# The last job of each output phase taken tile by tile in two banks, with most of the sums of squares inside its products

## The reference

```
x = x + gated_deltanet_mixer(rms_norm(x, a_norm_g), a_w_in, ...)      # phases A and OUT_A
x = x + moba_mixer(rms_norm(x, b_norm_g), b_w_in, w_out, kb, vb, ...) # phases B and OUT_B; kb, vb from rms_norm(x, kv_norm_g) @ w_kv
x = rms_norm(x, final_norm_g)
h = rms_norm_f32(x, norm_g) * (1 + scale) + shift                     # shift, scale, gate = silu(c) @ ada_w + ada_b
x = x + gate * retention_mixer(h, ...)                                # phases C and OUT_C
h = rms_norm_f32(x, norm_g) * (1 + scale) + shift
x = x + gate * chunked_attention_mixer(h, ...)                        # phases D and OUT_D
```

## Time and profile before

| | us |
|---|---|
| median of 3 runs | 833.12 |
| lowest and highest run | 832.19, 843.05 |
| the profiled execution's own time | 833.37 |
| its span | 831.5 |
| TensorE busy in the span | 814.4 |
| VectorE busy | 603.0 |
| ScalarE busy | 486.6 |
| GpSimd busy | 43.6 |

### The profile page before, as it was taken

The page is one execution under the profiler, slowest core; times in us unless marked ns, Lnnn a source line. Parts: engine busy times, 40 slices in busy tenths (PEclk is TensorE's granted clock), DMA queues, the critical chain, the costliest instruction groups (busy, mean ns, idle before and its releaser), DMA issues.

```text
span 831.5 us, 17292 instructions
## 1 busy us (share of the span) xinstructions
PE 814.4 (98%) x7278; PEld 793.7 (95%) x7278; DVE 603.0 (73%) x1049; ACT 486.6 (59%) x761; POOL 43.6 (5%) x68
## 2 busy tenths in 40 slices
PE   8999999999999999999999999989999999999998
PEld 7899999989999999999999999989999999999998
DVE  4776976678887876878797985556777867565662
ACT  5756756646855466553535354347777767677731
POOL 0500000018000100000000001000000000000000
PEclk9999999999999999999999999999999999999999
DMA  7363234526866884386666664973555644443450
GB/s 289 113 240 110 103 108 149 148 82 218 252 227 236 224 328 153 109 296 208 248 208 248 222 236 127 247 232 107 203 199 203 207 149 153 152 166 140 152 178 26
DMA packets 26493, 153.78 MB, mean 185 GB/s; under 512 B 2848, under 2 KB 3376, under 8 KB 12080
## 3 DMA queue, kind: packets, MB, share of 16 engines
q1 hardware_dynamic: 24432, 146.37, 50.3%
q0 software_dynamic: 1984, 6.31, 4.0%
HBM read 150.04 MB, written 2.62 MB: 184 GB/s over the span
## 4 chain that ended last, share of the span: by engine, by line
PE 84%; DVE 7%; DMA 4%; ACT 3%; issue 1%; SPq 0%; DVEq 0%; ACTq 0%
PE ps L489 83%; DMA raw<-weights 4%; DVE wlo L1444 3%; ACT whi L1013 1%; PE ps L869 1%; DVE early L1629 0%; DVE hlo L1472 0%; DVE arena L1476 0%; DVE early L1511 0%; DVE arena L1511 0%; DVE arena L1652 0%; DVE ada_ring L1525 0%; DVE olo L1489 0%; ACT hhi L1043 0%; PE ps L738 0%
## 5 line engine op out<-in xcount | busy, mean ns | idle before, releaser
L1444 DVE TENSOR_TENSOR wlo<-raw,whi 128x1024 fp32r<-128x1024 f32 x224 | 267.7, 1232 | 113.8 <-ACT whi L1013 113.8
L489 PE MATMUL ps<-hhi,whi 128*128 128x256 f32 x1024 | 295.0, 288 | 5.3 <-DVE hlo L1472 1.7
L489 PE MATMUL ps<-hlo,whi 128*128 128x256 f32 x1024 | 290.2, 283 | 0.0
L489 PE MATMUL ps<-hhi,wlo 128*128 128x256 f32 x1024 | 290.1, 283 | 0.0
L1013 ACT ACTIVATE whi<-raw 128x1024 fp32r<-128x1024 f32 x224 | 227.1, 1054 | 88.2 <-PE ps L489 60.9
L489 PEld LDWEIGHTS ps<-hhi,whi 128*128 128x128 f32 x1024 | 196.5, 192 | 8.2 <-issue 5.3
L489 PEld LDWEIGHTS ps<-hlo,whi 128*128 128x128 f32 x1024 | 196.7, 192 | 0.4
L489 PEld LDWEIGHTS ps<-hhi,wlo 128*128 128x128 f32 x1024 | 196.6, 192 | 0.0
L489 PE MATMUL ps<-ohi,whi 128*128 128x256 f32 x448 | 128.8, 287 | 1.4 <-DVE olo L1489 1.3
L489 PE MATMUL ps<-olo,whi 128*128 128x256 f32 x448 | 126.7, 283 | 0.0
L489 PE MATMUL ps<-ohi,wlo 128*128 128x256 f32 x448 | 126.7, 283 | 0.0
(11 more groups left out here) (232 smaller groups left out, 961.4 us busy)
## 6 DMA issues: line engine op xcount, KB each, us to landing
raw<-weights SPq DMA_DIRECT2D x112, 1024.0 KB, 5.0
ada_ring<-ada SPq DMA_DIRECT2D x24, 1024.0 KB, 5.1
arena<-bias_rows_d POOLq DMA_DIRECT2D x4, 512.0 KB, 15.8
x<-x_t SPq DMA_DIRECT2D x2, 512.0 KB, 4.7
arena<-bias_rows_b POOLq DMA_DIRECT2D x4, 256.0 KB, 7.8
bias_rows_d<-turns POOLq DMA_DIRECT2D x1, 1024.0 KB, 13.3
arena<-bias_rows_d POOLq DMA_DIRECT2D x4, 256.0 KB, 19.5
out_t<-x SPq DMA_DIRECT2D x4, 256.0 KB, 2.4
```

What stands on the lines that cost most here:

```text
L489: return pe.matmul(o, l, r, start=start, stop=stop, skip_group_check=skip)
L1444: dve.tensor_tensor(wlo[:, unit % UNITS, :, :], raw[:, c % RAW, 4 * half:4 * half + 4, :], whi[:, unit % UNITS, :, :].bitcast(F32), ALU.su ...
```

## The change

The last job of every output phase (19, 39, 67 and 103) is done by a new function, `job_by_tiles`. In its last chunk it takes all 24 products of tile 6 first, into the usual bank, and counts up tile_done; then the 24 of tile 7, into bank ps[6]. The units' slots are counted free in the second tile's products: the first unit's after k = 3 of tile 7, the second's at the end. VectorE adds tile 6 when tile_done comes, and tile 7 when the job is complete, each as one 128x256 instruction. ScalarE squares tile 6 on x6_ok and tile 7 on bank_free.

`x_sums` is split: `x_sums_begin` (ones products of tiles 0, 1 and 6) is issued in the last job behind its products k = 5 of tile 7, so that 6 products of the job come after it; `x_sums_end` (tile 7) stands where x_sums stood. The first unit of the chunk after the next moves: on VectorE from ahead of the addition to behind the addition of tile 7, on ScalarE from ahead of the squares to between the squares of tile 6 and tile 7. The low parts of the next chunk stay ahead of both additions. At the end tiles 6 and 7 of the result leave in a transfer each. Cut to its core:

```diff
-            for n in range(4):
+            for n in range(3):
                 J = JOB_OUT_D + n
                 sp.wait_ge(bank_free[J % 2], J // 2 - 5)
                 sp.dma_start(out[:, 2 * n:2 * n + 2, :], x[:, 2 * n:2 * n + 2, :]).then_inc(out_ok_sem, 16)
-            sp.wait_ge(out_ok_sem, 64)
+            sp.wait_ge(x6_ok_sem, 4)
+            sp.dma_start(out[:, 6, :], x[:, 6, :]).then_inc(out_ok_sem, 16)
+            sp.wait_ge(bank_free[(N_JOBS - 1) % 2], (N_JOBS - 1) // 2 - 5)
+            sp.dma_start(out[:, 7, :], x[:, 7, :]).then_inc(out_ok_sem, 16)
+            sp.wait_ge(out_ok_sem, 80)
...
+            def x_sums_begin(n):
+
+                pe.wait_ge(ss_read_sem, own_ss[0])
+                pe.wait_ge(xsq_add_sem, 2 * n)
+                pe.wait_ge(sq_ok_sem, 5 * n + 1)
+                for t in (0, 1, 6):
+                    mm(ssb[:, 0:S], ones[:, :], xsq[:, t, :], t == 0, False)
+
+            def x_sums_end(n):
+
+                pe.wait_ge(sq_ok_sem, 5 * n + 2)
+                mm(ssb[:, 0:S], ones[:, :], xsq[:, 7, :], False, True).then_inc(ss_ok_sem, 1)
+                own_ss[0] += 1
+
+            def job_by_tiles(J, between=None):
+
+                banks = (pj[J % 2], ps[6])
+                bank_empty(J)
+                cs = chunks_of(J)
+                for n, c in enumerate(cs):
+                    last = n == len(cs) - 1
+                    for t, k in [(t, k) for t in range(2) for k in range(KT)] if last else [(None, k) for k in range(KT)]:
+                        unit = 2 * c + k // 4
+                        if k % 4 == 0:
+                            pe.wait_ge(lo_ok_sem, unit + 1)
+                        for tile in range(2) if t is None else (t,):
+                            for a, (ws, hs) in enumerate(((whi, ohi), (whi, olo), (wlo, ohi))):
+                                m = mm(banks[tile][:, 0:S], ws[:, unit % UNITS, k % 4, tile * P:tile * P + P], hs[:, 8 * n + k, :],
+                                       n == 0 and k == 0 and a == 0, last and k == KT - 1 and a == 2)
+                        if t == 0 and k == KT - 1:
+                            m.then_inc(tile_done_sem, 1)
+                        elif t != 0 and k % 4 == 3:
+                            m.then_inc(w_units_sem, 1)
+                        if t == 1 and k == 5 and between is not None:
+                            between()
...
-            for J in range(JOB_OUT_A + 2, JOB_B):
-                job(J, "T", ohi, olo)
-
-            def x_sums(n):
-                pe.wait_ge(xsq_add_sem, 2 * n)
-                sums(lambda t: xsq[:, (0, 1, 6, 7)[t], :], 4, S, sq_ok_sem, lambda t: 4 * n - 2 + (3, 3, 4, 4)[t])
...
-                        job(J, "T", *h_q, ready=0, ready_sem=xg_lo_sem, at={4: lambda: x_sums(1)})
+                        job(J, "T", *h_q, ready=0, ready_sem=xg_lo_sem, at={4: lambda: x_sums_end(1)})
...
-            for J in range(JOB_OUT_B + 2, JOB_C):
-                job(J, "T", ohi, olo)
-
+            job(JOB_OUT_B + 2, "T", ohi, olo)
+            job_by_tiles(JOB_OUT_B + 3, lambda: x_sums_begin(2))
             ada_group(0)
-            x_sums(2)
+            x_sums_end(2)
...
-                    job(J, "T", ohi, olo)
-                ada_after(J)
+                    job_by_tiles(J, lambda: x_sums_begin(3))
             ada_group(1)
-            x_sums(3)
+            x_sums_end(3)
...
                     if n == 3:
-                        high(chunks_of(J0 + 4)[0] + 1, range(1))
+                        for t in (6, 7):
+                            if t == 6:
+                                act.wait_ge(x6_ok_sem, (JOB_OUT_A, JOB_OUT_B, JOB_OUT_C).index(J0) + 1)
+                            else:
+                                high(chunks_of(J0 + 4)[0] + 1, range(1))
+                                bank_taken(act, J)
+                            if J0 == JOB_OUT_A:
+                                act.activation(hhi[:, t, :], x[:, t, :], ACT.Copy, scale=col("b_norm", t)).then_inc(xg_hi_sem, 1)
+                            act.activation(xsq[:, t, :], x[:, t, :], ACT.Square, scale=1.0 if gain is None else gain(t)).then_inc(sq_ok_sem, 1)
+                        continue
...
-                        dve.wait_ge(sq_ok_sem, 4 * i + 2 + n)
+                        dve.wait_ge(sq_ok_sem, 5 * i + 2 + n)
...
-                    if n == 3 and J0 < JOB_OUT_D:
-                        low(chunks_of(J0 + 4)[0] + 1, range(1))
+
+                    def add_tile(t):
+
+                        k = 2 * n + t
+                        summed = ps[6][:, 0:S] if n == 3 and t else bank(J)[:, t, :]
+                        if gate is None:
+                            return dve.tensor_tensor(x[:, k, :], summed, x[:, k, :], ALU.add)
+                        return dve.scalar_tensor_tensor(out=x[:, k, :], in0=summed, scalar=mod[:, gate + k:gate + k + 1], in1=x[:, k, :], op0=ALU.mult, op1=ALU.add)
+
+                    def low_of_next(t):
+
+                        dve.wait_ge(xg_hi_sem, t + 1)
+                        dve.scalar_tensor_tensor(out=hlo[:, t, :], in0=x[:, t, :], scalar=col("b_norm", t), in1=hhi[:, t, :].bitcast(F32), op0=ALU.mult, op1=ALU.subtract).then_inc(xg_lo_sem, 1)
+
+                    if n == 3:
+                        i = (JOB_OUT_A, JOB_OUT_B, JOB_OUT_C, JOB_OUT_D).index(J0)
+                        dve.wait_ge(tile_done_sem, i + 1)
+                        add_tile(0).then_inc(x6_ok_sem, 1)
+                        if J0 == JOB_OUT_A:
+                            low_of_next(4)
+                            low_of_next(5)
+                            dve.wait_ge(x6_ok_sem, i + 1)
+                            low_of_next(6)
+                        sums_done(J)
+                        add_tile(1).then_inc(bank_free[J % 2], 1)
+                        if J0 == JOB_OUT_A:
+                            dve.wait_ge(bank_free[J % 2], J // 2 - 5)
+                            low_of_next(7)
+                        if J0 < JOB_OUT_D:
+                            low(chunks_of(J0 + 4)[0] + 1, range(1))
+                        continue
...
```

More of the change, by code:

```diff
@@ L358, in two_blocks @@
         ada_in_sem = sem("ada_in")
+        tile_done_sem = sem("tile_done")
+        x6_ok_sem = sem("x6_ok")
         bank_free = [sem(f"bank_free{i}") for i in range(2)]
@@ L530, in sums @@
                 for t in range(n):
-                    if cnt_sem is not None:
-                        pe.wait_ge(cnt_sem, cnt(t))
+                    pe.wait_ge(cnt_sem, cnt(t))
                     m = mm(ssb[:, 0:width], ones[:, :], src(t), t == 0, t == n - 1)
@@ L832, in _ @@
             ada(ADA_EARLY - 1)
-            for J in range(JOB_OUT_A + 2, JOB_B):
-                job(J, "T", ohi, olo)
-            def x_sums(n):
-                pe.wait_ge(xsq_add_sem, 2 * n)
-                sums(lambda t: xsq[:, (0, 1, 6, 7)[t], :], 4, S, sq_ok_sem, lambda t: 4 * n - 2 + (3, 3, 4, 4)[t])
+            job(JOB_OUT_A + 2, "T", ohi, olo)
+            job_by_tiles(JOB_OUT_A + 3, lambda: x_sums_begin(1))
             def head_sums(i, k):
@@ L980, in _ @@
                     job(J, "T", ohi, olo, split=8, at={4: lambda: sums_c(3)})
-                else:
-                    job(J, "T", ohi, olo)
-                ada_after(J)
+                elif J < JOB_D - 1:
+                    job(J, "T", ohi, olo)
+                else:
+                    job_by_tiles(J, lambda: x_sums_begin(3))
             ada_group(1)
-            x_sums(3)
+            x_sums_end(3)
             keep_warm(8)
@@ L991, in _ @@
                     job(J, "T", ohi, olo, split=16, at={8: turn_last, 12: mix_last})
+                elif J < N_JOBS - 1:
+                    job(J, "T", ohi, olo)
                 else:
-                    job(J, "T", ohi, olo)
+                    job_by_tiles(J)
         @block.scalar
@@ L1733, in add_x @@
                             low(J0 + 2, range(1, 2))
[L1734 to L1739, removed]
-                    else:
[L1741 to L1744, removed]
+                        if J0 == JOB_OUT_A and n:
+                            dve.wait_ge(bank_free[(J - 1) % 2], (J - 1) // 2 - 5)
+                            low_of_next(2 * n - 2)
+                            low_of_next(2 * n - 1)
+                    else:
+                        add_tile(0)
+                        add_tile(1).then_inc(bank_free[J % 2], 1)
             def attend(J0, pairs, soft0, bias, normed):
```

## The result

The changed kernel takes 838.53 us (median; 833.18 to 842.53 over 20 executions), the kernel before 833.25 us (830.49 to 843.05, 20 executions) beside it. The ratio is 1.0059, 95% interval 1.0046 to 1.0072: slower by 4.9 us, within 2%. The forecast was 838.7 us. The profiled execution of the changed kernel took 838.07 us, 835.9 of it in the span; that of before 833.37 and 831.5, so the spans differ by 4.4 us.

A forecast was written before the change was run, and what follows sets the result against it. The prediction took TensorE to bound the kernel, busy in 814.4 of 831.5 us. Its terms summed as 833.37 + 2.4 + 1.2 + 0.6 - 0.6 + 1.7 = 838.7 us, range 834.5 to 841.8.

The forecast's parts named there:

- The wait: In the last jobs of OUT_A, OUT_B and OUT_C, TensorE stands 3.2, 1.2 and 3.3 us for tile 6's square.
- OUT_A: End of OUT_A: the new wait, no longer covered by 24 products of B's first job, costs 2.4 us.
- OUT_B: End of OUT_B: TensorE never stood still there before, so the new wait is added whole, costing 1.2 us.
- The clock: Behind a long stall the granted clock falls once, taken at OUT_C, and slower instructions cost 1.7 us more.
- OUT_C: End of OUT_C: the earlier demand eats the gain meant there, costing 0.6 us without a clock fall.
- Rival 4: At OUT_C weights land 3.3 us sooner, removing stall and clock fall: no slower, 833.6 us; chance 0.10.
- The end: End of OUT_D: one shorter addition left and a smaller last transfer gain 0.6 us.
- Rival 3: At the output phases' ends, tile 6's additions come in time, nothing stalls: -4.2 us, 829.2 us; chance 0.05.

The follow-up runs named there:

- e1: Changed kernel with VectorE's addition of tile 6 ahead of the next chunk's low parts, and ScalarE's square ahead of its second high part: 830.04 us, ratio to before 0.9962.
- e2: Changed kernel with the ones sums of tiles 0, 1 and 6 put back behind the last job, additions still late: 830.59 us, ratio to before 0.9973.
- e7: Changed kernel with the edits of both e1 and e2: 829.5 us, ratio to before 0.9963.
- e4: Changed kernel with unneeded ones products on TensorE ahead of x_sums_begin in OUT_A, OUT_B and OUT_C (22, 8, 20 instructions): 842.74 us, ratio to before 1.0103.
- e8: Changed kernel with 16 unneeded ones instructions on TensorE ahead of x_sums_begin in OUT_A alone: 845.74 us, ratio to before 1.014.
- e10: Changed kernel run again with no edit, one execution, for a second trace: 838.31 us.
- e11: Changed kernel run again with no edit, one execution, for a third trace: 840.34 us.
- e3: Kernel before with only job 103 done tile by tile, tiles 6 and 7 added and sent apart: 832.47 us, ratio to before 1.0002.
- e6: Kernel before with only the third unit of OUT_A, OUT_B and OUT_C moved behind the last job's additions and squares: 832.55 us, ratio to before 0.9987.
- e9: Kernel before with the edits of e6 and e3 together: 830.38 us, ratio to before 0.997.

## Why the prediction was right, and where not

**The wait.** Right. It was foretold at three places with 3.2, 1.2 and 3.3 us, and is there with 2.83, 1.00 and 2.50, released by the square each time, with tile 6 added when the second wlo ends. e1, e2 and e7 remove it from either side and remove the loss.

**OUT_A.** +2.4 foretold without a fall of the clock, +2.28 and +2.29 with the stall filled (e4, e8). The cover named is the 24 products that now stand behind the wait. e2 shows it: its additions are as late, its sums wait behind those products again, and TensorE does not stand still there.

**OUT_B.** +1.2 foretold, +1.23 measured in all three traces of the changed kernel.

**The clock.** The step that failed is its place, "I take one such fall, at OUT_C": for the term of 1.7 us there the runs show 0. Of the ends of the output phases, one had a fall, OUT_A. The price of 1.7 us was near in the profiled execution (1.38) and in e10 (14.47 - 12.94 = 1.53), and too low in e11 (15.67 - 12.94 = 2.73). I had argued from the old fall at OUT_C and from the stall being longest there. The stall came out shorter there than at OUT_A (2.50 against 2.83), and the old fall stays with the old order (before and e3). That reading also said that the old trace had one fall; it has a second, from 46 to 50, in phase A. The Trainium skill, TensorE: Matmul & The Clock Gate, section "HAM oscillation — how this bites in real kernels", describes a loop that waits some 3 to 5 us for data between groups of matmuls and starts each group throttled again; the 3.2 and 3.3 us foretold lay at the lower end of that. In this case's traces shorter stalls go with a fall at OUT_A, three times of three with 2.83 us, and not at OUT_C of the changed order with 1.25 to 3.02 us, none of four. What sets the two apart stays open. The length of the stall alone does not: 1.58 and 1.74 us at OUT_C of the old order went with a fall, 3.02 us did not.

**OUT_C.** +0.6 without a fall foretold, and -0.07 came. The working took "everything on VectorE and ScalarE up to there as before", but there ScalarE waits for weights, and they came sooner: the second wlo ended 12.5 us behind job 66's addition before (540.16 to 552.69), 12.0 after. In e11 and e8, with the same VectorE list, OUT_C is 16.22 and 18.28. So this term moves by 1.2 us down and 0.8 up between traces of one VectorE list, and should have had that as its bounds. Rival 4 needed 3.3 us sooner; 0.5 came.

**The end.** -0.6 foretold, -0.68 here and -0.71 in e3.

**The sum.** 5.3 us foretold; 4.4 in the spans, of which 0.62 lies ahead of the change. At the places themselves: 3.66 + 1.23 - 0.07 - 0.68 = 4.14; e10 and e11 give 4.2 and 4.3. The forecast is 0.2 us off the median, and that is luck: the fall came, but at another place, OUT_C's other 0.6 us did not, and the medians differ by 5.3 us (4.9 by the ratio) where the three traces find 4.1 to 4.3 at the places. What makes up the rest isn't known.

**Where the meant gain went.** Rival 3 put it at -4.2 us if the additions came in time, 0.8 of it at OUT_A and 2.8 at OUT_C. e1 gets just that at the places (-0.80, -3.07, end -0.64), and gives 0.5 us back in B. The timeline of e1 shows where. One product starts 0.57 us behind the one ahead of it, where its neighbours stand 0.12 apart; the kernel before has no such gap there, e2 has it too. The profile names nothing that it waits for:

```profile
211.89 0.36 PE L495 MATMUL ps<-ohi,whi 128*128 128x256 f32 x1 [0.29 <-issue]
```

By the places of e6 and e9 nearly all of it comes from the third unit, which the change did move behind the additions; in the times it shows for e9 (0.997) and not for e6 alone. e2 shows that the changed kernel held this gain, and that the wait ahead of six products spent it. The sums inside the job earn nothing that the times can show: e7, which lacks them, is as fast as e1, which has them. OUT_C is 0.57 shorter with them (14.46 against 15.03), in one trace each.

## What to carry to other kernels

Before an instruction is moved ahead on an in-order engine, follow its inputs back through the lists of the other engines: what counts is when they are issued there, not when they could be. Work that stood behind the wait and now stands ahead of it was cover. First put the urgent short operation ahead of the preparing long ones on the engines that feed it, and only then ask for its result earlier; here the first half, with the split end (e9), gave 0.3%, and no version that asks earlier is faster beyond the intervals.

## What the runs showed of the hardware that was not expected

- The time of an execution goes with its mean granted clock. For the changed kernel 833.18 us stand at a mean granted clock of 1.000, 835.16 at 0.998, 838.07 to 840.0 at 0.994 and 840.06 to 842.53 at 0.990. Besides OUT_A, falls come early in the program at places that differ from run to run (72 to 76 and 110 to 114 in the profiled execution; only 46 to 50 that early in the old one; none in e1). TensorE was busy in all of 68 to 72, ahead of the first of these, so such a fall costs time without a long stall in the rows next to it. By the starts in the table one more fall is worth 1 us or a little more, an estimate.
- One fall can last twice as long as another. In the profiled execution that at OUT_A is over by 206; in e11 it went on for some 6 us while TensorE was busy, and cost 2.73 us, twice the 1.38. e3 (554 to 560), e4 (297 to 303) and e8 (74 to 80) have one as long. Stretches of e11:

```profile
204.00:206.00 2.00, 0.96 (x2) 0.53 0.59 131
206.00:208.00 2.00, 2.00 (x7) 0.50 0.97 397
208.00:210.00 2.00, 2.00 (x11) 0.50 1.07 238
210.00:212.00 2.00, 2.00 (x15) 0.76 1.04 184
```

- In e4 a weight transfer was asked for 0.46 us behind another engine's write instead of with it, and its user waited 5.61 us. B was 7.19 us longer, more than the change itself cost. It is one trace, and the cause isn't shown.
